# The last block of an MLP's second projection as two jobs of half the tokens each, with the final norm's first half in the second job

## The reference, cut to what matters

```python
def rmsnorm(x, g):
    xf = x.astype(jnp.float32)
    var = jnp.mean(xf * xf, axis=-1, keepdims=True)
    return (xf * lax.rsqrt(var + NORM_EPS) * g.astype(jnp.float32)).astype(x.dtype)

def squared_relu_mlp(xn, w_ff1, w_ff2):
    h = jax.nn.relu(jnp.einsum('bsd,df->bsf', xn, w_ff1))
    return jnp.einsum('bsf,fd->bsd', h * h, w_ff2)

# second_block, its end
        xn = rmsnorm(h, norm_mlp_g[l])
        h = h + squared_relu_mlp(xn, w_ff1[l], w_ff2[l])
    return rmsnorm(h, norm_final_g)
```

## Time and profile before

| what | us |
|---|---|
| median of 3 timed runs | 3513.41 |
| lowest and highest of them | 3508.55, 3515.98 |
| profiled execution, first to last instruction (its span) | 3518.9 |
| TensorE busy in it | 3127.7 (89%) |
| VectorE busy | 1393.3 (40%) |
| ScalarE busy | 927.4 (26%) |

### The profile page before, as it was taken

The page is one execution under the profiler, slowest core; times in us unless marked ns, Lnnn a source line. Parts: engine busy times, 40 slices in busy tenths (PEclk is TensorE's granted clock), DMA queues, the critical chain, the costliest instruction groups (busy, mean ns, idle before and its releaser), DMA issues. The chain is left out here.

```text
span 3518.9 us, 35593 instructions
## 1 busy us (share of the span) xinstructions
PE 3127.7 (89%) x14452; PEld 2319.9 (66%) x14452; DVE 1393.3 (40%) x2157; ACT 927.4 (26%) x1476; POOL 189.5 (5%) x250
## 2 busy tenths in 40 slices
PE   7997777999898876887884998999999899999998
PEld 7786744566676663332332877888777688888887
DVE  3126846884444334111115647531215423333334
ACT  3432335663334210000003131021322232222222
POOL 0001012110000001111112000000000000000000
PEclk8998978999999987999996999999999899999999
DMA  3111000003220046999994132111112111111112
GB/s 96 45 48 9 6 13 1 1 1 119 68 84 7 30 200 243 420 421 419 412 401 196 38 71 59 58 54 48 33 57 90 42 43 52 51 48 48 48 48 78
DMA packets 140067, 370.02 MB, mean 105 GB/s; under 512 B 45888, under 2 KB 59840, under 8 KB 113920
## 3 DMA queue, kind: packets, MB, share of 16 engines
q1 hardware_dynamic: 129552, 346.97, 26.8%
q0 software_dynamic: 9216, 16.80, 1.3%
q10 hardware_dynamic: 1152, 4.19, 0.3%
HBM read 352.70 MB, written 32.83 MB: 110 GB/s over the span
## 5 line engine op out<-in xcount | busy, mean ns | idle before, releaser
L2606 PE MATMUL moe_ph<-moe_wgu,moe_rowsT 128*64 128x512 f32 x1024 | 266.3, 680 | 65.8 <-DMA moe_wgu<-in_moe_w_up_dram 35.6
L590 PE MATMUL mlp_ps<-mlp_high,mlp_w_cut 128*128 128x512 f32 x1024 | 316.7, 391 | 2.6 <-PEq L274 2.6
L590 PE MATMUL mlp_ps<-mlp_w_cut,mlp_hidden_high 128*128 128x512 f32 x1024 | 315.2, 389 | 0.0
L482 DVE TENSOR_TENSOR m_w_cut<-m_w_raw,m_w_cut 128x512 fp32r<-128x512 f32 (+1 forms) x86 | 80.8, 940 | 431.3 <-ACT m_w_cut L478 431.1
L2606 PEld LDWEIGHTS moe_ph<-moe_wgu,moe_rowsT 128*64 128x64 f32 x1024 | 85.3, 155 | 226.5 <-issue 204.9
L482 DVE TENSOR_TENSOR mlp_w_cut<-mlp_w_raw,mlp_w_cut 128x1024 fp32r<-128x1024 f32 x63 | 77.2, 1225 | 396.1 <-ACT mlp_w_cut L478 395.7
L590 PEld LDWEIGHTS mlp_ps<-mlp_high,mlp_w_cut 128*128 128x128 f32 x1024 | 193.0, 189 | 43.1 <-issue 3.0
L590 PEld LDWEIGHTS mlp_ps<-mlp_w_cut,mlp_hidden_high 128*128 128x128 f32 x1024 | 192.2, 188 | 39.9
L478 ACT ACTIVATE m_w_cut<-m_w_raw 128x512 fp32r<-128x512 f32 (+1 forms) x86 | 71.4, 830 | 516.2 <-PE m_gates_ps L590 192.8
L478 ACT ACTIVATE mlp_w_cut<-mlp_w_raw 128x1024 fp32r<-128x1024 f32 x63 | 66.7, 1059 | 525.2 <-PE mlp_ps L590 523.6
L590 PE MATMUL mlp_ps<-mlp_low,mlp_w_cut 128*128 128x512 f32 x512 | 199.7, 390 | 0.0
(11 more groups left out here) (548 smaller groups left out, 6018.6 us busy)
## 6 DMA issues: line engine op xcount, KB each, us to landing
moe_wgu<-in_moe_w_gate_dram SPq DMA_DIRECT2D x64, 1024.0 KB, 22.0
moe_wgu<-in_moe_w_up_dram SPq DMA_DIRECT2D x64, 1024.0 KB, 27.0
moe_wd<-in_moe_w_down_dram SPq DMA_DIRECT2D x64, 1024.0 KB, 19.7
mlp_w_raw<-in_w_ff_dram SPq DMA_DIRECT2D x64, 512.0 KB, 3.3
m_w_raw<-in_w_in_dram SPq DMA_DIRECT2D x48, 256.0 KB, 2.8
mix_w_raw<-in_w_in_dram SPq DMA_DIRECT2D x40, 256.0 KB, 2.6
m_w_raw<-in_w_in_dram SPq DMA_DIRECT2D x20, 512.0 KB, 3.5
x_w_raw<-in_x_w_kv_dram SPq DMA_DIRECT2D x16, 512.0 KB, 3.5
```

Source lines behind the costliest of these rows:

```text
L482: nc.vector.tensor_tensor(part(s, 1).bitcast(F32R), raw(s), part(s, 0), ALU.subtract).then_inc(low_ready, 1)
L590: ins = nc.tensor.matmul(ps[:, b, :r.shape[-1]], l, r, start=(k == 0 and sw is high and wh == 0), stop=(k == job.nk - 1 and sw is low))
L2606: ins = self.nc.tensor.matmul(self.ps_h[r, i].rearrange("p (i n) -> p i n", i=2), self.rowsT[:, i, k, r], self.wgu[:, w * self.parts + h, ...
```

## The change

The last block, down 7, becomes two other jobs. Job a computes tiles 0 to 3 with all 1024 columns, job b tiles 4 to 7. In both, bank b holds tile b//2 of the half and column half b%2. Their pieces are "wide": one row block of 128 rows and 1024 columns, which is again 128x1024 elements and 512 KB, but is used for only 24 matmuls (8 banks x 1 row block x 3). Each job has 4 such pieces, and both load and cut the same weights. All the other jobs stay as they are.

The final norm is split. ScalarE squares and roots tiles 0 to 3 at the first piece of job b (ahead of its cut of the third piece of b), and tiles 4 to 7 after all its cuts. VectorE scales tiles 0 to 3 (`first_half`) right after the eight additions of job a, ahead of its low cut of the second piece of b. Tiles 4, 5 and 6 are scaled after the additions of banks 3, 5 and 7 of job b, tile 7 at the end. The gain is loaded at the beginning of the projection, ahead of the third piece. The stores stay behind the last load of weights.

```diff
     def pieces(self, jobs):
-        return [(i, k, j.w[:, k:k + self.kp]) for i, j in enumerate(jobs) for k in range(0, j.nk, self.kp)]
+        step = lambda j: 1 if j.wide else self.kp
+        return [(i, k, j.w[:, k:k + step(j)]) for i, j in enumerate(jobs) for k in range(0, j.nk, step(j))]
+
+    def shaped(self, place, w):
+        if w.shape[-1] > CH:
+            return place.rearrange("p k n -> p (k n)")[:, 0:w.shape[-1]].unsqueeze(1)
+        return place[:, :, :w.shape[-1]]
...
@@ project, at its start
+        if tail:
+            tail.added, tail.before = emptied["vector"], banks * (sum(j.engine == "vector" for j in jobs) - 2)
...
@@ project, serve
-            for s, (i, k, _) in enumerate(pieces):
-                job, last = jobs[i], k + kp == jobs[i].nk
+            for s, (i, k, w) in enumerate(pieces):
+                job, last = jobs[i], k + w.shape[1] == jobs[i].nk
                 if side:
                     (side.scalar if mine == "scalar" else side.vector)(eng, s)
+                if tail and mine == "scalar" and i == len(jobs) - 1 and k == 0:
+                    tail.scalar(eng, 0)
...
                         if tail and s == n - 1:
                             tail.vector(eng, b)
+                    if tail and i == len(jobs) - 2:
+                        tail.first_half(eng)
                     if job.then:
                         job.then()
                 if s + cuts < n:
...
             if tail and mine == "scalar":
-                tail.scalar(eng, emptied["vector"], banks * order[-1])
+                tail.scalar(eng, 1)
...
@@ project, sync
+                    if s == 2 and tail:
+                        tail.fetch(sp)
                     if s >= 2 + precut:
                         sp.wait_ge(low_ready, s - 1 - precut)
                     stream.load(sp, s, pieces[s][2])
...
@@ project, tensor
-                        for j in range(kp):
+                        for j in range(piece.shape[1]):
...
                                     l, r = sw[:, k, job.tokens(b)], w[wh][:, j]
+                                    if job.wide:
+                                        r = r[:, (b % 2) * CH:(b % 2 + 1) * CH]
...
@@ mlp_second
+            w = a["w_ff2_2"][0, j * CH:(j + 1) * CH]
+            jobs = add_halves(hidden[j % 2], w, x) if j + 1 == n else add_jobs(c, hidden[j % 2], w, x)
...
+        def add_halves(src, w, x):
+            def half(h):
+                def evacuate(b, ps):
+                    at = x[:, 4 * h + b // 2, (b % 2) * CH:(b % 2 + 1) * CH]
+                    return nc.vector.tensor_tensor(at, ps, at, ALU.add)
+
+                return Job(columns(w, 0, D), True, src, evacuate, "vector", wide=True,
+                           tokens=lambda b: slice((4 * h + b // 2) * P, (4 * h + b // 2 + 1) * P))
+
+            return [half(h) for h in range(2)]
...
@@ FinalNorm
-    def scalar(self, act, added, before):
+    def scalar(self, act, h):
-        for m in range(NT):
-            act.wait_ge(added, before + m + 1)
+        for m in range(4 * h, 4 * h + 4):
+            act.wait_ge(self.added, self.before + 2 * (m + 1))
...
+    def first_half(self, dve):
+        for m in range(4):
+            self.scale(dve, m)
+
     def vector(self, dve, b):
         if b is None:
-            for m in range(NT - 2, NT):
-                self.scale(dve, m)
-        elif b >= 2:
-            self.scale(dve, b - 2)
+            self.scale(dve, NT - 1)
+        elif b >= 3 and b % 2:
+            self.scale(dve, 4 + b // 2 - 1)
...
-    def sync(self, sp):
+    def fetch(self, sp):
         sp.dma_start(self.gain[:], self.a["norm_final_g_2"].unsqueeze(0).to_broadcast([P, D])).then_inc(
             self.gain_in, 16)
+
+    def sync(self, sp):
         for m in range(NT):
             sp.wait_ge(self.scaled, m + 1)
             sp.dma_start(self.out[:, m], self.x[:, m]).then_inc(self.c.stored, 16)
```

More of the change, by code:

```diff
@@ L390, in __init__ @@
     def __init__(self, w, rows, src, evacuate, engine, tokens=None, then=None, finish=None, after=0,
-                 ready=None):
+                 ready=None, wide=False):
         self.w, self.rows, self.evacuate, self.engine, self.then = w, rows, evacuate, engine, then
@@ L394, in __init__ @@
         self.tokens = tokens or (lambda b: slice(b * P, (b + 1) * P))
+        self.wide = wide
 class Stream:
@@ L406, in load @@
     def load(self, sp, s, w):
-        sp.dma_start(self.raw[:, s % 2, :, :w.shape[-1]], w).then_inc(self.c.arrived[s % 2], 16)
+        sp.dma_start(self.shaped(self.raw[:, s % 2], w), w).then_inc(self.c.arrived[s % 2], 16)
     def pieces(self, jobs):
-        return [(i, k, j.w[:, k:k + self.kp]) for i, j in enumerate(jobs) for k in range(0, j.nk, self.kp)]
+        step = lambda j: 1 if j.wide else self.kp
[4 more added lines that the diff above has]
+        return place[:, :, :w.shape[-1]]
     def begin(self, sp, jobs):
@@ L419, in first_pieces @@
     def first_pieces(self, w):
-        return self.raw[:, 0, :, :w.shape[-1]], [self.cut[:, 0, i, :, :w.shape[-1]] for i in range(2)]
+        return self.shaped(self.raw[:, 0], w), [self.shaped(self.cut[:, 0, i], w) for i in range(2)]
     def first_high(self, act, jobs, ready):
@@ L468, in part @@
         def part(s, which):
-            return stream.cut[:, s % cuts, which, :, :pieces[s][2].shape[-1]]
+            return stream.shaped(stream.cut[:, s % cuts, which], pieces[s][2])
         def raw(s):
-            return stream.raw[:, s % 2, :, :pieces[s][2].shape[-1]]
+            return stream.shaped(stream.raw[:, s % 2], pieces[s][2])
         def make_high(act, s):
@@ L566, in _ @@
             def _(pe):
-                for s, (i, first, _) in enumerate(pieces):
+                for s, (i, first, piece) in enumerate(pieces):
                     job = jobs[i]
@@ L3757, in down @@
         def down(j):
-            jobs = add_jobs(c, hidden[j % 2], a["w_ff2_2"][0, j * CH:(j + 1) * CH], x)
+            w = a["w_ff2_2"][0, j * CH:(j + 1) * CH]
+            jobs = add_halves(hidden[j % 2], w, x) if j + 1 == n else add_jobs(c, hidden[j % 2], w, x)
             jobs[0].after = 8 * (j + 1)
             return jobs
+        def add_halves(src, w, x):
[6 more added lines that the diff above has]
+            return [half(h) for h in range(2)]
         n = DFF // CH
```

## The result

| | before | changed |
|---|---|---|
| median of 20 runs, us | 3512.94 | 3519.74 |
| lowest and highest | 3508.0, 3524.29 | 3510.62, 3524.97 |
| profiled execution's span | 3518.9 | 3508.9 |

The ratio is 1.0018, with a 95% interval of 1.0011 to 1.0026: slower by 6.3 us, interval 3.9 to 9.1 (the two medians themselves lie 6.8 apart). The forecast was +4.2. The change adds time, by an amount near the bound of 0.2% that this kernel's scatter allows one to tell from nothing.

What follows compares the result with a forecast made beforehand. TensorE was taken to bound the kernel up to the last piece of weights, VectorE from there on. Stall +4.0, clock +1.7 and tail -1.5 gave +4.2 on a median of 3513.4: 3517.6 us, range 3510.5 to 3524.

Steps and rivals of the forecast that it cites:

- T: Moment when the last product of the next-to-last job, job a after the change, is there; claimed not to move.
- The new wait: Four scalings on VectorE delay the low cut of job b's second piece; TensorE stalls 4.0 us, bounds 2.6 to 5.4.
- The clock: After the stall TensorE's granted clock falls to 0.50 for 3.4 to 3.7 us; price 1.7, bounds 0 and 2.7.
- The tail: End of job b: last scaling 6.53 us behind the last product instead of 8.01; gain 1.5, bounds 0.9 and 1.7.
- After the stall: Job b's later cuts and loads and the first half's four stores arrive in time; cost nothing.
- Rival E: Job b's last load shares the queue with four stores and runs late; part of the 0.05 for anything else.
- Gain and table loads: Earlier gain load at the projection's start costs nothing; a possible 1.28 us ScalarE table load before the first root, not counted.
- The sum: Stall +4.0, clock +1.7, tail -1.5: +4.2 us on the profiled execution and on the median; forecast chance 0.74.
- the same: Whole kernel: a change within some 0.2% (7.0 us) cannot be told from no change; chance 0.80.
- B: Last block: the stall comes without a fall of the clock; +2.5 us, 3515.9; chance 0.12.
- D: Job b after its first piece: the clock stays low to the end; +15.5 us, 3529; chance 0.04.
- C: Last block: no stall of TensorE, only the tail's gain of 1.5 us is left; 3511.9; chance 0.05.

Runs made afterwards that it cites:

- e0_after: The changed kernel run again without any edit; ratio 1.0020 (1.0011 to 1.0029) against the kernel before.
- e2_halves_only: The changed kernel with both half jobs, but all of the final norm after job b's cuts; ratio 1.0006 (0.9994 to 1.0017) against the kernel before.
- e1_cut_first: The changed kernel with VectorE's low cut of job b's second piece ahead of the first half's four scalings; ratio 0.9996 (0.9987 to 1.0005) against the kernel before.

## Why the prediction was right

*T stays.* 676.39 from the MLP's start to T against 676.60; the a-pieces stalled nowhere.

*The new wait.* The step that decided held. Predicted from T: first square 1.00, first reciprocal 2.50, VectorE free at 8.06, low cut's end 9.29. Measured (T = 3471.67): 1.03, 2.59, 8.17, and TensorE at work at 9.45. The additions ended 0.3 earlier than said and, as said, the first root set the start, not they: VectorE waited 0.86 for it. Stall 4.0 predicted; 4.04 of gap and 0.30 of restarting, which I had at 0.16 and counted inside the 4.0. So the 4.0 was small by 0.3: 0.19 in the gap, for which 3.85 had been worked out, and 0.14 in the restart.

*The clock.* 1.7 predicted, 1.6 in four of five traces and 2.2 in the fifth. It fell each time. The Trainium skill ("TensorE: Matmul & The Clock Gate", section "HAM oscillation — how this bites in real kernels") prices such a loss as the throttled time times one half. Applied to the part of the throttled time in which TensorE worked, 3.41 would by that rule cost 1.7 and the 4.78 of e0_after 2.4; the traces agree within 0.2, with 1.6 and 2.2.

*The tail.* Last scaling 6.53 behind the last product predicted; 6.49 behind the end of the last matmul measured, where the kernel before has 8.06 by the same two records (8.01 in the prediction). Gain 1.6, predicted 1.5. Its pattern held too: ScalarE's last root was exposed, and VectorE waited for it before tile 7. The end of the changed kernel on ScalarE and VectorE:

```profile
3504.00 0.29 ACT L3827 ACTIVATE fin_rstd<-fin_ssq,eps 128x1 f32<-128x1 f32 x1
```

```profile
3504.33 0.16 DVE L3847 RECIPROCAL fin_rstd<-fin_rstd 128x1 f32<-128x1 f32 x1 [0.15 <-ACT fin_rstd L3827]
3504.53 1.28 DVE L3849 SCALAR_TENSOR_TENSOR x<-x,fin_rstd,fin_gain 128x1024 f32<-128x1024 f32 x1
```

*After the stall* one number was wrong and cost nothing. I had b3's load, issued ahead of the four stores, land after 3.1. Issues between 3480.5 and 3490, with their time to landing:

```profile
out_dram<-x SPq DMA_DIRECT2D x4, 512.0 KB, 6.0
mlp_w_raw<-in_w_ff_dram SPq DMA_DIRECT2D x1, 512.0 KB, 5.7
```

It took 5.7, and 5.7 to 6.0 in the five traces. It landed at 3486.8, and b3's high cut was due at 3488.54, after b1's products, so it lacked 1.7 us to reach ScalarE's cut, and more to reach TensorE. Rival E put such a delay down to the four stores. They are the smaller part of it. In e2_halves_only, where the first store is issued 17.6 us behind b3's load, that load still took 5.0, and the two ahead of it 3.2 each. The load of b3 in e2_halves_only, with what else moved in its window:

```profile
q8 instruction: 1, 0.02, 1.3%
mlp_w_raw<-in_w_ff_dram SPq DMA_DIRECT2D x1, 512.0 KB, 5.0
```

So the stores cost it 0.7 to 1.0, and 1.8 are there without any. Where these come from stays open: one instruction packet of 16 KB moved in that window and none in the windows of the two loads ahead, but no run tests it. The first half's stores had all landed by T+20.1 to T+20.4, not by T+18, still 7 us ahead of the second half's.

*Gain and table loads.* The gain landed 3.9 after its issue at 2795.23, the cut behind it went off at 2808.06 without waiting for a load; no table load stands between ScalarE's copies and roots, so the 1.28 that I weighed was not paid.

*The sum.* +4.2 predicted, +4.3 in four traces: 4.3 for the stall, 1.6 for the clock and -1.6 for the tail, so most of the 0.3 that the stall had too little is made up by the clock, which cost 0.1 less, and the tail, which gained 0.1 more. That closeness is in part luck. The three timings say 6.3, 7.0 and 3.5; the forecast's 1.0012 lies in all three intervals, near the lower end of two. The first, 0.18%, lies just inside the 0.2% that I had called the same. The rivals: B and D seen in none of five traces, C is what e1_cut_first looks like, and only with its edit.

## What to carry to other kernels

Work that is moved into another job is hidden only if it stands behind everything on its engine that the bounding engine still needs, or fits into the time that is left until that is due: list what is queued behind the moved work, with the time at which each item is due. By the gaps of 1.25, 2.65 and 4.04, one scaling ahead of the cut would have cost nothing (an estimate, 1.25 less 1.39; not run). Here one 1.2 us cut stood behind four scalings and turned a gain of 1.6 into a loss of 4.3. Where pieces get shorter, every chain that had one piece's length as its cover must be counted again, and a stall of TensorE costs more than its length: 4.0 of gap came to 5.9.

## What the runs showed of the hardware beyond that

A gap of 1.25 us in otherwise dense matmuls left the clock at 1.00, in one trace; gaps of 2.65 and 4.04 did not, in six traces of six. VectorE instructions with two inputs in SBUF took longer beside GpSimd: a scaling 1.98 instead of 1.28, once, and products of 128x1024 2.09 to 2.38 instead of 1.21 to 1.22, in twelve traces. And a 512 KB load with four stores of the same size issued within 4.5 us behind it landed after 5.7 to 6.0; the same load took 5.0 with no store near it, and the two loads ahead of it there 3.2.
